# A mixture-of-experts layer on one core: the experts' rows gathered as quarter rows and turned by VectorE in 32x32 blocks

## What is computed

```python
def grouped_moe(x, router_w, router_b, w_gate, w_up, w_down):
    probs = jax.nn.softmax((xf @ router_w).astype(jnp.float32) + router_b.astype(jnp.float32), axis=-1)
...
    def expert_block(args):
        xb, e = args
        hdn = jax.nn.silu(xb @ w_gate[e]) * (xb @ w_up[e])
        return hdn @ w_down[e]
...
def reference(...):
    mix = hybrid_mixer(x, w_in[l], b_in[l], conv_w[l], mh_norm_g[l], w_out[l])
    x = layer_norm(ALPHA * x + mix, ln_mix_g[l], ln_mix_b[l])
    ffn = grouped_moe(x, router_w, router_b, w_gate[l], w_up[l], w_down[l])
    x = layer_norm(ALPHA * x + ffn, ln_moe_g[l], ln_moe_b[l])
```

## Time and profile before

| | us |
|---|---|
| median of three runs | 1663.07 |
| fastest, slowest of them | 1660.44, 1663.07 |
| span of the profiled execution | 1660.3 |
| stage of the experts, first gate matmul to the end | 972.7 to 1660.3 |
| one expert, 4 to 5, between the same transposes | 41.1 |

### The profile page before, as it was taken

The page is one execution under the profiler, slowest core; times in us unless marked ns, Lnnn a source line. Parts: engine busy times, 40 slices in busy tenths (PEclk is TensorE's granted clock), DMA queues, the critical chain, the costliest instruction groups (busy, mean ns, idle before and its releaser), DMA issues. The chain is left out here.

```text
span 1660.3 us, 24919 instructions
## 1 busy us (share of the span) xinstructions
PE 1600.5 (96%) x9446; PEld 1387.7 (84%) x9446; DVE 1084.1 (65%) x1838; ACT 662.7 (40%) x936; POOL 340.3 (20%) x270
## 2 busy tenths in 40 slices
PE   8999999999999999999999579999999999999994
PEld 6888888888888888888888479999999999999993
DVE  4536867647767468676477766664676667666776
ACT  3224424144333243251442434443555455545552
POOL 2100015100044000071000012212232333232333
PEclk9999999999999999999999879999999999999997
DMA  7422335322535322444225436665777777777762
GB/s 243 147 82 77 134 120 203 103 81 98 178 104 176 102 77 93 161 165 140 76 77 200 177 124 205 214 213 154 237 252 251 227 239 250 248 226 240 250 212 99
DMA packets 119350, 276.28 MB, mean 166 GB/s; under 512 B 15632, under 2 KB 17808, under 8 KB 118720
## 3 DMA queue, kind: packets, MB, share of 16 engines
q1 hardware_dynamic: 92544, 187.63, 33.0%
q0 software_dynamic: 26112, 84.95, 17.1%
q10 hardware_dynamic: 576, 2.10, 0.3%
HBM read 229.66 MB, written 48.40 MB: 167 GB/s over the span
## 5 line engine op out<-in xcount | busy, mean ns | idle before, releaser
L1279 PE MATMUL mix_acc<-kept_xT,mix_w_high 128*128 128x512 f32 x640 | 256.8, 401 | 2.9 <-DVE mix_w_low L1093 2.9
L1281 PE MATMUL mix_acc<-kept_xT,mix_w_low 128*128 128x512 f32 x640 | 251.2, 393 | 0.0
L1280 PE MATMUL mix_acc<-kept_xT,mix_w_high 128*128 128x512 f32 x640 | 250.3, 391 | 0.0
L937 DVE TENSOR_TENSOR mix_w_low<-mix_w_raw,mix_w_high 128x2048 fp32r<-128x2048 f32 x71 | 164.3, 2313 | 107.2 <-ACT mix_w_high L750 107.0
L750 ACT ACTIVATE mix_w_high<-mix_w_raw 128x2048 fp32r<-128x2048 f32 x71 | 135.9, 1915 | 233.1 <-PE mix_acc L1281 233.1
L1940 DVE TENSOR_TENSOR moe_gate_up_low<-kept_w_gate_up_raw,moe_gate_up_high 128x2048 fp32r<-128x2048 f32 x64 | 146.6, 2290 | 75.3 <-ACT moe_gate_up_high L1789 75.2
L2313 PE MATMUL moe_gate_psum<-moe_xT_high,moe_gate_up_high 128*128 128x288 f32 x512 | 154.7, 302 | 1.4 <-DVE moe_xT_low L1965 1.4
L2315 PE MATMUL moe_up_psum<-moe_xT_high,moe_gate_up_low 128*128 128x288 f32 x512 | 152.3, 297 | 0.0
L2314 PE MATMUL moe_gate_psum<-moe_xT_low,moe_gate_up_high 128*128 128x288 f32 x512 | 152.0, 297 | 0.0
L2314 PE MATMUL moe_up_psum<-moe_xT_low,moe_gate_up_high 128*128 128x288 f32 x512 | 151.9, 297 | 0.0
L2313 PE MATMUL moe_up_psum<-moe_xT_high,moe_gate_up_high 128*128 128x288 f32 x512 | 151.7, 296 | 0.0
(11 more groups left out here) (482 smaller groups left out, 3396.6 us busy)
## 6 DMA issues: line engine op xcount, KB each, us to landing
mix_w_raw<-in_w_in SPq DMA_DIRECT2D x56, 1024.0 KB, 5.2
kept_w_gate_up_raw<-in_w_gate SPq DMA_DIRECT2D x32, 1024.0 KB
kept_w_gate_up_raw<-in_w_up SPq DMA_DIRECT2D x32, 1024.0 KB
queries_keys_or_down_raw<-in_w_down SPq DMA_DIRECT2D x32, 1024.0 KB, 9.6
mix_w_raw<-in_w_out SPq DMA_DIRECT2D x16, 1024.0 KB, 5.0
kept_conv_or_residual<-in_x POOLq DMA_DIRECT2D x16, 512.0 KB, 5.5
mix_x_rows<-in_x POOLq DMA_DIRECT2D x12, 512.0 KB, 4.4
x<-kept_conv_or_residual POOLq DMA_DIRECT2D x12, 512.0 KB, 2.9
```

The source lines that it names most:

```text
L937: dve.tensor_tensor(wl[:, stage % 2], raw[:, stage % 2], wh[:, stage % 2].bitcast(F32), ALU.subtract).then_inc(split_l, 1)
L1279: pe.matmul(out, ah, bh, start=first, stop=False)
L1280: pe.matmul(out, ah, bl, start=False, stop=False)
L1281: return pe.matmul(out, al, bh, start=False, stop=last)
```

## The change

A row of 1024 floats is now gathered in quarters of 256. Each expert's 288 slots form nine blocks of 32 slots, four in A, four in B and one in U. For block m one indirect DMA fills 128 partitions with 1 KB each: partition 32 j + i gets quarter j of the row of slot i. That makes nine gathers for an expert in place of three. A 32x32 turn in each quarter of the partitions then brings channels to the partitions: DVE's `transpose` (`turn`, L1972 of the new kernel) takes every eighth float of a quarter row, so that partition p holds channels 8 p to 8 p + 7, and one instruction turns a whole tile. PE's transposes are gone. Since partition p now holds eight neighbouring channels, `w_gate` and `w_up` are loaded with eight neighbouring rows to a partition ("(p c) n"), in pieces of 8 KB in place of 2 KB.

`x_high` and `x_low` read the turned tiles from SBUF, in three instructions in place of five; `x_low` of A stands behind `h_low` of the last quarter. Tile A is turned into memory of its own, B and U into the memory of the low parts. The sigmoid goes straight into the hidden tile. The indices of the quarter rows need the slot numbers on other partitions: a product on PE with `keep.repeat`, now 128 x 128, spreads them, and DVE makes indices from it, before the first gather can start. `down_last` waits for less, and the averaging at the very end uses `keep.repeat` in place of a tile of its own.

```diff
@@ load_gate_up
-        src = w.rearrange("(c p) n -> p c n", p=P)
+        src = w.rearrange("(p c) n -> p c n", p=P)
@@ experts, tiles
-    ROWS = (P, P, UT)
+    BLOCKS = (range(0, 4), range(4, 8), range(8, 9))
+    PAIRS = 2 * NE
+    NIDX = 4 * PAIRS + NE
...
-        X = sb("x_rows", [P, COLS, D])
-        xTh, xTl = (sb(n, [P, KC, CAP], F32R) for n in ("xT_high", "xT_low"))
-        sig = sb("sigmoid", [P, CAP])
+        X = sb("x_quarter_rows", [P, CAP // UT, DQ])
+        XA = sb("xT_first_tile", [P, KC, P])
+        xTh = sb("xT_high", [P, KC, CAP], F32R)
+        with nc.sbuf_tensor("moe_xT_other_tiles", [P, KC, CAP], F32) as XT:
+            pass
+        xTl = sb("xT_low", [P, KC, CAP], F32R)
...
-        xT_at = (px, (pg[0], pu[0]), px[0:1])
-        PARTS = (2, 2, 1)
-        X_OPS = sum(PARTS)
@@ gpsimd
+            x_quarters = x1_dram.rearrange("s (q n) -> (s q) n", q=QUARTERS)
+
             def gather(r, e, k):
 
-                n = ROWS[k]
-                pool.indirect_dma_start(out=X[0:n, k], out_offset=None, in_=x1_dram,
-                                        in_offset=bass.IndirectOffsetOnAxis(
-                                            ap=gather_i[0:n, COLS * e + k:COLS * e + k + 1], axis=0))\
-                    .then_inc(x_in[k], 16)
+                for m in BLOCKS[k]:
+                    at = 4 * PAIRS + e if k == U else m % 4 * PAIRS + 2 * e + k
+                    pool.indirect_dma_start(out=X[:, m], out_offset=None, in_=x_quarters,
+                                            in_offset=bass.IndirectOffsetOnAxis(ap=gather_i[:, at:at + 1], axis=0))\
+                        .then_inc(x_in[k], 16)
...
-                    wait_apart(pool, idle, x_ps[k], r * NE + e + 1)
+                    wait_apart(pool, idle, turned[k], r * NE + e + 1)
@@ scalar
-            def x_high(r, e, k, part):
+            def x_high(r, e, k):
                 if e == NE:
                     return
-                act.wait_ge(x_ps[k], r * NE + e + 1)
-                if e:
+                act.wait_ge(turned[k], r * NE + e + 1)
+                if e and k == A:
                     act.wait_ge(gu_used, r * (NE * FC) + e * FC)
-                n = KC // PARTS[k]
-                act.activation(xTh[:, part * n:(part + 1) * n, AT[k]],
-                               xT_at[k][part][:, 0:n * ROWS[k]].rearrange("p (c n) -> p c n", c=n), ACT.Copy)\
-                   .then_inc(xh_done, 1)
+                src = XA[:] if k == A else XT[:, :, AT[k]]
+                act.activation(xTh[:, :, AT[k]], src, ACT.Copy).then_inc(xh_done, 1)
@@ vector
+            def turn(r, e, k):
+
+                if e == NE:
+                    return
+                blocks = BLOCKS[k]
+                landed = 16 * len(blocks)
+                wait_apart(dve, idle, x_in[k], r * (NE * landed) + (e + 1) * landed)
+                if e and k == A:
+                    wait_apart(dve, idle, xl_done, r * (NE * COLS) + (e - 1) * COLS + 1)
+                elif e:
+                    wait_apart(dve, idle, gu_used, r * (NE * FC) + e * FC)
+                rows = X[:, blocks[0]:blocks[-1] + 1].rearrange("p m (d b) -> p m b d", b=KC)
+                to = XA[:] if k == A else XT[:, :, AT[k]]
+                dve.transpose(to.rearrange("p b (m i) -> p m b i", i=UT), rows).then_inc(turned[k], 1)
...
             def tables(r):
-                own.step(dve.tensor_scalar(tok[:, 0], psl[:, 0:NCOL], -1.0, 0.0, ALU.add, ALU.max))
-                own.wait(r)
-                dve.tensor_copy(gather_i[:], tok[:, 0]).then_inc(gather_ready, 1)
...
+                own.step(dve.tensor_tensor(spread_in[:, 0:4 * PAIRS].rearrange("p (m e k) -> p m e k", m=4, k=2),
+                                           by_pair.unsqueeze(1).to_broadcast([P, 4, NE, 2]),
+                                           mask.to_broadcast([P, 4, NE, 2]), ALU.mult))
...
+                dve.wait_ge(last_ps, r + 1)
+                own.step(dve.tensor_scalar(quarter_of, psu[:, 0:NIDX], 4.0, keep.quarter[:, 0:1], ALU.mult, ALU.add))
+                own.wait(r)
+                dve.tensor_scalar(gather_i, quarter_of, keep.block[:, 0:1], None, ALU.max).then_inc(gather_ready, 1)
...
                 tables(r)
+                turn(r, 0, A)
                 rounds_needed(r)
                 backs(r)
+                for k in range(1, COLS):
+                    turn(r, 0, k)
                 for k in range(COLS):
-                    for part in range(PARTS[k]):
-                        x_low(r, 0, k, part)
+                    x_low(r, 0, k)
+                turn(r, 1, A)
...
                     h_low(r, e, 2)
+                    if e:
+                        turn(r, e + 1, A)
...
                     row_norm(r, e - 1, 1 if e == LAST else 0)
                     hidden(r, e, FC - 1)
-                    x_low(r, e + 1, A, 0)
+                    turn(r, e + 1, B)
+                    turn(r, e + 1, U)
                     h_low(r, e, FC - 1)
-                    x_low(r, e + 1, A, 1)
-                    for part in range(2):
-                        x_low(r, e + 1, B, part)
+                    for k in range(COLS):
+                        x_low(r, e + 1, k)
@@ tensor
-                        if f == FC - 2:
-                            turn_x(r, e + 1, A)
-                    turn_x(r, e + 1, B)
...
                         down(r, e, A)
-                        turn_x(r, e + 1, U)
                         down(r, e, B)
                         down_last(r, e)
```

115 lines of the change are left out of this document (47 added, 68 removed).

## The result

The changed kernel takes 1704.08 us (median of four runs, 1702.98 to 1708.02), where the kernel before takes 1663.07 (1660.44 to 1663.52): a ratio of 1.0259, 95% interval 1.0243 to 1.0275. It is slower by 2.6%. The profiled execution spans 1702.6 us, 42.3 more than before, against a forecast of 14.6 less.

A forecast was written before the change was run, and what follows sets the result against it. PE was taken as the bound in the expert stage, busy 50.00 of 50 us. 1660.3 - 37.5 + 14 + 7.9 + 1 = 1645.7 us profiled, put on the median as 1648.5 us; range 1638 to 1674, forecast's own 1639 to 1658.

The forecast's parts named there:

- chain ahead of the first expert: Before the expert loop: index product, quarter gathers, turns and splitting delay the first matmul by 7.9 us (5 to 11).
- clock in the first expert: At the first expert's start: PE idles beforehand, so the lower clock lasts 1 us more (0 to 3).
- transposes off PE: In experts 1 to 15: PE loses its transposes, 2.5 us an expert, 37.5 us less in all.
- waits on the hidden tile's low part: In the expert loop: PE waits on DVE for the fourth hidden tile's low part, 14 us more in all.
- The turn's duration: On DVE, each expert: three turns taken as 1.14, 1.14 and 0.35 us, with the double as the other end.
- rival 1: On DVE: strided turns cost double and DVE becomes the bound; 1681 us, slower, deciding from about 4.6 us; chance 0.17.
- the step called hidden: In the expert loop: nine gathers' issue, scatters queued behind and DMA delay nobody; nothing taken, up to 10 us in the range.
- rival 3: In 14 experts: quarter-row gathers hold up the weights by up to 0.7 us each; 1658 us; chance 0.08.
- Rival 2: In the expert loop: PE's clock falls in five new waits, costing 5 x 1.7 us; 1657 us; chance 0.07.
- the detour of the indices: Before the first gather: a PE product and two more DVE steps, bounded by 1.5 and 3 us, taken as 2.1.
- after 985: Sign of being wrong: the first gate matmul comes after 985, where near 981 was expected.

The follow-up runs named there:

- a_flat: a_addr with turns reading neighbouring channels and weights loaded as in the changed kernel, so its products are not the layer's: 1652.46 us, ratio 0.9952.
- the probe: Layer's computation left out; timed VectorE turns and subtractions at steps of 1, 2, 4 and 8 floats, and TensorE matmuls at six operand placements: turns 1.26 to 2.26 us.
- a_pool: a_addr with GpSimd's order changed: scatter of A ahead of the gathers of the next B, scatters of B and U ahead of U's gather: 1682.62 us, ratio 1.0138.
- b_shift: The kernel before with one unused tile of 32 bytes a partition ahead of the down weights' tile, two small tiles merged for room: 1675.98 us, ratio 1.0081.
- probe2: Layer's computation left out; timed 512-column TensorE matmuls for thirteen placements of the two operands: steps of 0.227 to 0.233 us.
- a_addr: The changed kernel with its new small tables folded into spare places, so the mixer's large tiles begin where they did before: 1691.67 us, ratio 1.0190.
- a_late_pool: a_pool with the turn of U ahead of the fourth hidden tile's low part and that of B behind it, step of eight floats kept: 1655.68 us, ratio 0.9966.
- a_best: a_late_pool with round counting ahead of A's first turn, A's low part before B's turn, and A's turn later in two-row-tile experts: 1644.41 us, ratio 0.9875.
- a_flat_late_pool: a_late_pool with the contiguous turns of a_flat, so its products are not the layer's: 1641.46 us, ratio 0.9901.
- a_pad: The changed kernel with one unused tile of 32 bytes a partition ahead of the down weights' tile: 1694.03 us, ratio 1.0183.

## Why the prediction was wrong

The two profiled executions differ by 42.3 us. By its own terms:

| term | forecast | measured | from |
|---|---|---|---|
| mixer | 0 | +14.6 | the slot table's matmuls, 956.90 and 971.52 |
| chain ahead of the first expert | +7.9 | +9.5 | 996.84 - 972.74 - 14.6 |
| clock in the first expert | +1 | +0.6 | its period less the loop's and its wait: 2.3 after, 1.7 before |
| transposes off PE | -37.5 | -37.2 | 15 x (41.13 - 38.65), the period of a_flat |
| waits on the hidden tile's low part | +14 | +39.3 | the view of waits, 38.2 + 1.1 |
| clock at its lower level behind waits | 0 | +12 | six experts of 38.65 + wait + 1.8 to 2.9, less the next row |
| restart behind a wait | 0 | +3.4 | 0.25 in each of 14 experts |
| clock in expert 3, and the end | 0 | 0 | -1.6 and +1.6 |

In expert 3 the clock falls in both kernels while PE is busy all the time (0.50 from 1115 to 1119 before); nothing here shows why.

**The transposes** were right: 2.5 us an expert, a period of 38.6.

**The turn's duration** is the step that failed first: the three turns of an expert take 4.8 us, not 2.6, and with them the term "14 us more" of waits was mis-sized. Forecast and measured spans differ by 57 us; 39 of them go with the stride. I took 1.14, 1.14 and 0.35 us from DVE's subtractions, and set aside the double because L2117 shows nothing of a stride. The turns took 2.2, 2.0 and 0.6: 4.8 in all, past the 4.6 from which rival 1 was to decide. The pair of L2117 and L2128 was no test: sixteen elements in an instruction of 175 ns, where the effect to be seen was 17 ns and the probe shows it for 1024. Door 1 of "SBUF — State Buffer" in the Trainium skill spoke against the change, and the probe's 2.26 us bear it out. A rule that speaks against a change, and that the trace cannot refute at the size in question, ought to have had more than 0.17.

**The waits.** The chain was right: with turns of 1.24 us (a_flat) PE waits 2.3 us in experts 7, 9, 11 and 13, where I had said 2.5, and hardly in those with one tile or none. With the true turns these waits are 4.2 in a_pool, and all of them 32.3: 18 of the 25 us that were missing, 7 more where the down weights are late. The rest of the 5.92 is the step called hidden: "queued behind them are the scatters and the list rows; the next users are a whole period away". The scatter of A, issued 6.4 us ahead of the next expert before, now came between 5.5 us ahead and the start itself. The down weights, whose load was also issued late, landed later, and their splitting, and all of DVE's row behind it, came up to 1.7 us late. It was near to rival 3, with other weights than I had named; a_pool prices the order on GpSimd at 9 us (1691.67 - 1682.62), 1.2 of them ahead of the first expert. What in that order does it is open, as said above.

**The clock.** Rival 2 had the price of a fall near enough, 1.7 us, where 1.6 were measured behind the shorter waits and up to 2.7 behind those over 5 us. But it stood as a case by itself, where it goes with rival 1: longer waits bring more falls. A fall lasts 3.4 or 6.8 us, and not by the wait alone: behind equal waits of 4.2 us a_pool has both. Rival 1 with 39 us of waits in place of 44, a better figure for its chain, 12 us of clock, 3.4 of restarts and the mixer's 14.6 comes to some 1705 on the median; its own 1681 had neither clock nor mixer.

**Ahead of the first expert**, step by step: the detour of the indices 1.8 us (977.66 - 961.26 - 14.6; taken 2.1); A's last piece issued 3.9 after the first and landed 2.9 later (4.0 and 3); the turn 0.8 more than taken, the two later ones 1.0 more. The first gate matmul came "after 985", which was named as a sign of being wrong; without the mixer's 14.6 us it would have stood at 982.2.

**The mixer** was in no step. I had read the diff's tables for what they compute and not for their size. A difference of 96 bytes in `keep` moves every tile behind it, and b_shift shows that 32 are enough for 0.8%. The stretch that the prediction called the same in both kernels lost a third of the whole difference.

Beside these, the longer issue on POOL held nobody up directly (POOL is busy 25.6 of 50 us), its part in the late scatters aside, and a_flat, with everything of the change but the stride and the shift, took 1652.46 where 1648.5 were forecast for the whole.

## What to carry to other kernels

Take a stride's price from a row that has as many elements as the new instruction; a short one hides it in its fixed part. When a change alters the size of a small tile, ask what stands behind it, and compare the step of PE's matmuls in a stretch that the change doesn't touch. An operation moved to an engine beside the bound goes behind the result that the bound waits for, not ahead of it, and rivals that feed each other (a longer wait, a lower clock) are to be added, not listed side by side.

## What was not expected of the hardware

- PE's step for 512 columns is 0.227 us where its two operands stand a multiple of 256 bytes apart (0, 256, 512 and 1024 tried), and 0.229 to 0.233 at the other distances tried; a common shift doesn't matter (probe2, mixer).
- A step of two floats is free on VectorE (1.26 us for 1024 elements), one of four costs 2.04, one of eight 2.26; a turn that writes with a step of eight takes 2.2.
- Loads of weights onto 32 partitions ran at 170 GB/s (1.7 MB in 10 us), with gathers beside them; one of 256 KB whose source had four parts in its outermost dimension took SyncE 1.1 us (gate) or 2.6 (up) in the median to issue.
- A semaphore of PE rose 1.0 to 1.5 us after the next product's first matmul (up to 3.0 in a_addr) in place of 0.1, in seven experts of after and nine of a_addr, while PE ran on. What delays it isn't known.
- The clock fell behind every wait of 2.4 us of a_late_pool, behind four of the five of 2.3 to 2.9 in a_flat, and behind none of the ten of 1.2 and 1.4 in a_best and a_flat_late_pool. In after, a_pad, a_addr and a_pool, seven more waits are of 2.3 to 2.9 us, and it fell behind three of them. What decides it between equal waits isn't settled.
